# Two tiles of work moved on TensorE in each attention half of a two-layer encoder

## The reference

```
h = rms(x, attn_norm);  z = h @ w_in
dq, dk = rope(z[q part]), rope(z[k part]);  dv = z[v part]         # 4 heads of differential attention
c_q, c_kv, k_pe = z[256 columns], z[128 columns], z[64 columns]    # compressed q, compressed kv
a      = softmax(q1 @ k1) - lam * softmax(q2 @ k2)                 # per head: two maps of scores
y_diff = rms(a @ dv, diff_subln) * (1 - lam_init)
qh     = rms(c_q, q_a_norm) @ w_q_b                                # latent attention: 4 heads, nope 128 + rope 64
k_nope, v = rms(c_kv, kv_a_norm) @ w_kv_b
y_mla  = softmax(q_nope @ k_nope + q_pe @ k_pe) @ v
x = x + concat(y_diff, y_mla) @ w_o
x = x + (silu(h2 @ w_gate) * (h2 @ w_up)) @ w_down                 # h2 = rms(x, ffn_norm)
```

## Time and profile before

| | |
|---|---|
| median of 3 runs | 2397.21 us (2394.81 to 2398.03) |
| the profiled execution | 2398.18 us, of which its span is 2396.4 us |
| TensorE busy in the span | 2348.0 us (98%) |
| VectorE busy | 1752.5 us (73%) |
| ScalarE, GpSimd busy | 777.3 us (32%), 814.8 us (34%) |
| mean granted TensorE clock | 0.996 of full speed |

### The profile page before, as it was taken

How to read it: one execution, slowest core, us unless ns; L and a number is a source line. 1 busy time by engine, 2 the same in 40 slices (tenths; PEclk the granted TensorE clock), 3 DMA queues, 4 the chain that set the end, 5 groups by cost and what they waited for, 6 DMA issues and landing times.

```text
span 2396.4 us, 32372 instructions
## 1 busy us (share of the span) xinstructions
PE 2348.0 (98%) x11064; PEld 1947.1 (81%) x11064; DVE 1752.5 (73%) x3040; ACT 777.3 (32%) x1508; POOL 814.8 (34%) x615
## 2 busy tenths in 40 slices
PE   8999999999999999999999999999999999999997
PEld 6878888878888888888888788878888888888886
DVE  7988398777667777666758864887666666666677
ACT  4555145532222222222224532455222222222222
POOL 4314000156666666663300010001444444444321
PEclk9999999999999999999999999999999999999998
DMA  8624541354333343331332235223211111111122
GB/s 305 220 80 158 199 152 53 113 181 136 124 130 124 131 131 117 120 114 52 124 141 106 78 123 206 104 88 132 88 53 53 53 53 53 53 53 44 44 82 85
DMA packets 55104, 266.91 MB, mean 111 GB/s; under 512 B 6496, under 2 KB 6624, under 8 KB 36960
## 3 DMA queue, kind: packets, MB, share of 16 engines
q1 hardware_dynamic: 54288, 264.83, 32.1%
q10 hardware_dynamic: 720, 0.86, 0.1%
HBM read 196.45 MB, written 69.21 MB: 111 GB/s over the span
## 4 chain that ended last, share of the span: by engine, by line
PE 79%; DVE 10%; issue 3%; ACT 2%; POOL 0%; DVEq 0%; ACTq 0%; POOLq 0%
PE bank L482 25%; PE bank L484 25%; PE bank L483 25%; DVE x L1842 2%; PE bank L993 2%; DVE u_lo L1828 1%; PE bank L831 1%; DVE silu L1817 1%; PE bank L839 1%; DVE qpe L1663 0%; DVE aT_lo L1788 0%; ACT w L1460 0%; PE bank L489 0%; PE bank L488 0%; DVE x L1906 0%
## 5 line engine op out<-in xcount | busy, mean ns | idle before, releaser
L482 PE MATMUL bank<-h_hi,w 128*128 128x512 f32 x1792 | 702.7, 392 | 0.0
L484 PE MATMUL bank<-h_hi,w 128*128 128x512 f32 x1792 | 698.8, 390 | 0.0
L483 PE MATMUL bank<-h_lo,w 128*128 128x512 f32 x1792 | 698.5, 390 | 0.0
L1842 DVE TENSOR_TENSOR x<-x,bank 128x512 f32<-128x512 f32 x768 | 469.9, 680 | 3.1 <-PE bank L484 0.6
L692 POOL TENSOR_TENSOR w<-raw,w 128x512 fp32r<-128x512 f32 x230 | 333.2, 1473 | 327.3 <-ACT w L1367 115.9
L484 PEld LDWEIGHTS bank<-h_hi,w 128*128 128x128 f32 x1792 | 336.8, 188 | 70.3
L483 PEld LDWEIGHTS bank<-h_lo,w 128*128 128x128 f32 x1792 | 337.1, 188 | 68.7
L482 PEld LDWEIGHTS bank<-h_hi,w 128*128 128x128 f32 x1792 | 337.1, 188 | 68.5
L744 POOL TENSOR_TENSOR wd<-down_raw,wd 128x512 fp32r<-128x512 f32 x120 | 163.0, 1366 | 481.5 <-ACT wd L1453 481.5
L482 PE MATMUL bank<-u_hi,wd 128*128 128x512 f32 x560 | 220.5, 394 | 4.5 <-issue 2.1
L483 PE MATMUL bank<-u_lo,wd 128*128 128x512 f32 x560 | 218.3, 390 | 0.0
(11 more groups left out here) (213 smaller groups left out, 3948.0 us busy)
## 6 DMA issues: line engine op xcount, KB each, us to landing
w<-parked SPq DMA_DIRECT2D x81, 1024.0 KB, 4.8
raw<-in_wffn SPq DMA_DIRECT2D x88, 512.0 KB, 3.6
parked<-w SPq DMA_DIRECT2D x27, 1024.0 KB, 6.6
parked<-p SPq DMA_DIRECT2D x27, 1024.0 KB, 4.8
down_raw<-in_wffn SPq DMA_DIRECT2D x44, 512.0 KB, 3.7
raw<-in_watt SPq DMA_DIRECT2D x27, 512.0 KB, 4.4
praw<-in_watt SPq DMA_DIRECT2D x27, 512.0 KB, 5.7
x_kept<-x SPq DMA_DIRECT2D x4, 2048.0 KB, 9.9
```

The costliest lines, as they stand in the source:

```text
L482: nc.tensor.matmul(out_ap, lhs[0], rhs[0], start=first, stop=False)
L483: nc.tensor.matmul(out_ap, lhs[0], rhs[1], start=False, stop=False)
L484: return nc.tensor.matmul(out_ap, lhs[1], rhs[0], start=False, stop=last)
L1842: nc.vector.tensor_tensor(xn, xn, bank[banks + m][:], op).then_inc(s_acc.sem, 1)
```

## The change

Two entries of `TENSOR_ORDER` change their place; the tables of the other engines, all operations and all waits stay. The table is gone through in each of the four halves.

```
-    | S 13 | Pa cq1 | ST ckv | T 11 | Pb cq0 | S 14 | RB ckv | Pb cq1 | S 15 | ST cq | A 4 | T 12 | RB cq | T 13 | A 5
-    | T 14 | P kn0 | P pe0 | P qn0 | T 15 | ST y2 | A 6 | A 7 | S 16 | P vm0 | S 17 | P vm1 | P vm2 | RB y2 | S 18 | P
+    | S 13 | Pa cq1 | ST ckv | T 11 | Pb cq0 | S 14 | RB ckv | Pb cq1 | ST cq | S 15 | A 4 | T 12 | RB cq | T 13 | A 5
+    | T 14 | P kn0 | P pe0 | P qn0 | T 15 | ST y2 | A 6 | A 7 | S 16 | P vm0 | S 17 | P vm1 | S 18 | P vm2 | RB y2 | P
```

## The result

The changed kernel takes 2402.38 us, median of 18 runs (2400.07 to 2407.28), against 2396.91 us for the kernel before, 18 runs on the same chips (2394.81 to 2398.14): a ratio of 1.0026, interval 1.002 to 1.0033, or 5.5 us slower. The profiled execution took 2402.2 us with a span of 2400.4.

What follows compares the result with a forecast made beforehand. TensorE, busy 98% of the span, was taken as the bound, so only its waits count. 5.8 - 0.4 - 3.1 = +2.3 us on 2397.2 gave 2399.5 us, range 2396 to 2403.5.

Steps and rivals of the forecast that it cites:

- VectorE's order, not TensorE's, decides the first edit: Halves 2 to 4: `MX 15` and `AL ckv` stay ahead of `cq`'s chain, so `T 13` is 1.93 us late, 5.8 us in all.
- the wait of 0.87 us for the squares: Before `ST cq`, halves 2 to 4: TensorE newly idles 0.87 us until ScalarE has squared `cq1`.
- the one of 1.76 us for the root: Before `RB cq`, halves 2 to 4: TensorE's wait for the reciprocal root grows from 0.53 to 1.76 us.
- The second edit's gain: `S 18` ahead of `vm2`, all halves: 0.77 us left at `qn1`, four times, 3.1 us; bounds 0 and 1.23 us.
- the small new wait forecast before `qn1`: Before `qn1`, halves 2 to 4: a new small wait, expected as a sign in the profile after.
- the gain lasts: After `qn1`, halves 2 to 4: no TensorE wait above 0.2 us until their end, so the 0.77 us is kept.
- Half 1: At `ST cq` and `S 15`: `T 13` 0.6 us late, less 1.0 us from the clock, -0.4 us; bounds -1.0 and +0.9.
- I take the clock as staying up: Half 1, `RB cq`: after a wait of about 1.9 us the clock stays at 1.00, returning 1.0 us.
- The slow operation beside GpSimd: Half 1, `cq`'s root chain: the tiny operation of 1.21 us beside GpSimd goes; the chain needs about 2.4 to 2.5 us.
- a fall in halves 2 to 4: Sign that the prediction is wrong: TensorE's granted clock falls in halves 2 to 4.
- The rival: At `RB cq`, every half: the new waits bring the clock down, 1.0 us a time, 2403.5 us; chance 0.15.
- the rivals: Clock falls: 2403.5 us, chance 0.15; `S 18` move gives nothing: 2402.6, 0.1; `ST cq` move costs only its wait: 2396.3, 0.07.

Runs made afterwards that it cites:

- Experiment 3: Changed kernel, with `AL ckv` and `RQ cq` ahead of `MX 15` in VectorE's table: 2397.91 us, ratio 1.0003 to the kernel before.
- experiment 1: Kernel before, with only `ST cq` moved ahead of `S 15`: 2407.26 us, ratio 1.0044 to the kernel before.
- 4: Changed kernel, with the first map of `S 15` ahead of `ST cq` and the second behind it: 2398.31 us, ratio 1.0003 to the kernel before.
- experiment 6: Changed kernel, with the first map of `S 15` computed once more ahead of `ST cq`: 2399.63 us, ratio 1.0015 to the kernel before.
- experiment 2: Kernel before, with only `S 18` moved ahead of `vm2`: 2392.68 us, ratio 0.9985 to the kernel before.
- 7: As experiment 2, and `P kn0` moved ahead of `RB cq`: 2391.24 us, ratio 0.9978 to the kernel before.

## Why the prediction was right in part and wrong in part

- **VectorE's order, not TensorE's, decides the first edit: right.** 1.93 us was forecast for `T 13` and 1.93 measured in halves 3 and 4; the wait of 0.87 us for the squares is listed as 0.69, the one of 1.76 us for the root as 1.75. Experiment 3 shows the mechanism by undoing it.
- **The second edit's gain: right.** 0.77 us at `qn1`, forecast and measured; the small new wait forecast before `qn1` is not listed. The step "the gain lasts" was a little low: 0.98 us by `oa0`, and 4.6 us in all instead of 3.1, with an interval from 1.4 to 5.8 us that holds both.
- **Half 1: wrong.** "I take the clock as staying up" was the step, at -0.4 us for the first edit. `T 13` came 2.56 us late (11.75 against 9.19 us after `cq1`), where 0.6 was forecast, because the clock fell, at `ST cq` and not at `RB cq`. Before's fall behind the 2.77 us wait did go away, and this one, twice as long, took its place. As before's own fall came only behind its `T 13`, `oa0` is the fairer measure: 0.43 us late (48.61 against 48.18), where the two edits together were to make it 1.2 us early. In experiment 1, with a fall of 3.4 us there, the half came out 0.17 us early at `oa0`. The slow operation beside GpSimd is gone as forecast (in before there were two, of 1.21 and 1.18 us, now 0.17 and 0.16); the chain takes 2.39 us (8.24 to 10.63).
- **The clock in halves 2 to 4: the step that cost the forecast its likeliest case.** The prediction names a fall in halves 2 to 4 as a sign of being wrong, and half 2 has one. The rival had the right kind of loss, and its chance of 0.15 looks low after the fact. That its time, 2403.5 us, lies near 2402.4 is in part luck: it counted four falls of 1.0 us, the profile has two at this place, and the one in half 2 cost 2.16 us. It named the wrong place too: it watched the longest wait, and saw the short wait and the tiny matmuls ahead of it only as an addition. The waits of 1.75 us that it feared were followed by no fall in nine cases (two in the changed kernel, one in experiment 1, three each in 4 and 6). Sixteen one-column matmuls behind an idle stretch of 0.69 to 1.43 us brought one in 9 of 14 cases (in halves 2 to 4 alone in 4 of 9, in half 1 in 5 of 5); with no wait listed for the first of them in none of 18; thirty-two of them in 4 of 4. (Cases are halves of the profiled executions. In 9 of the 18, half 1 of before and of experiments 2 and 7, and halves 2 to 4 of experiments 4 and 6, the weight load ahead of them waited 0.43 to 0.49 us; in the 14 it waited 1.11 us or more.) Experiment 3's mean clock leaves open what part the wait for the root has in how often the clock falls.
- **The sum.** Forecast +2.3 us with no falls but for the clock's return in half 1; measured +3.1 us with the falls mostly taken away (experiment 6) and +5.5 us with them. The fixed part was forecast well within what the interval can tell; the time lies inside the range because the range took in the nearer part of the rivals.
- **What the profiled execution alone would have told**, +4.0 us in span, is no measure: at the entry to layer 0's FFN the kernel before waited 2.86 us and then ran at half clock, the changed one waited 1.69 us and did not. Over the nine profiles this wait runs from 0.65 to 2.86 us, though no edit touches the FFN, and after one of 2.82 us (experiment 2) the clock stayed at 1.00.

## What to carry to other kernels

Moving a producer ahead of other work helps nobody if the consumer's engine, in its own fixed order, still takes other work first; look up what stands ahead of the reader there, and count how much later that work now gets its input. Keep TensorE on full-width work ahead of a row of tiny matmuls, and keep the row short, since here sixteen were safe that way and thirty-two were not; judge such a row by the granted clock behind it, since busy shares and waits don't show that loss. When a reorder is worth a microsecond or two a time, split it into its edits and time each: here one of two gained 4.6 us (1.4 to 5.8) and the other lost 10 (7 to 14).

## What the runs showed of the hardware

- One-column matmuls (0.11 us apart, each with its 128-column weight load) are listed as busy, but with thirty-two of them in a row and no pause (3.6 us at full clock) the granted clock fell to 0.50 in four of four halves, in two while they ran and in two behind them.
- The same kernel's falls differ between halves that have the same instructions and the same waits to 0.01 us, and in length: 3.4, 6.8 or 10.2 us. One of 3.4 us cost 1.05 us at `T 13`, one of 6.8 us 2.16 us. What decides in which half it falls was not settled.
- A wait of 1.8 us before `oa0` in half 1 was followed by a fall in three of nine profiles (experiments 1, 4 and 6), and not in the kernel before; one row of one execution was too little to take the clock as safe.
